# A new order for a kernel's front part: queries last, a compression on four column tiles, and attention signalled branch by branch

## The reference, cut to what matters

```
h = rms_norm(x, norm1_w) * (1 + sc1) + sh1
q, kvs, gate_logits, b_gate, c_gate, u = split(h @ w_in)
k_c = rms_norm(silu(blocks(kv0) @ w1k) @ w2k);  v_c = silu(blocks(kv1) @ w1v) @ w2v
o = g0 * softmax(q k_c + bias) v_c + g1 * softmax(q k_s + bias) v_s + g2 * softmax(q k_w + bias) v_w
y_conv = b_gate * short_conv(c_gate * u, conv_w)
x = x + g1 * (rms_norm(concat(o, y_conv)) @ w_out)
```

## Time and profile before

| what | value |
|---|---|
| median of three runs | 1794.41 us |
| the profiled execution, its own time | 1793.89 us |
| its span in the trace | 1792.1 us |
| mean granted TensorE clock | 0.882 |
| PE busy | 1398.0 us (78%) |
| DVE busy | 611.7 us (34%) |
| bytes moved | 589.96 MB, mean 329 GB/s |
| chain that ended last | DMA 48%, PE 42%, DVE 5% |

### The profile page before, as it was taken

One profiled execution on the slowest core, in us unless ns is written; L12 is line 12 of the kernel. 1 busy time (PEld: TensorE's weight loads), 2 busy tenths in 40 slices (PEclk: granted clock), 3 DMA queues, 4 the chain that ended last, 5 costly groups with the idle time before them and its releaser, 6 DMA issues.

```text
span 1792.1 us, 24506 instructions
## 1 busy us (share of the span) xinstructions
PE 1398.0 (78%) x10619; PEld 860.1 (48%) x10619; DVE 611.7 (34%) x956; ACT 199.5 (11%) x439; POOL 5.0 (0%) x10
## 2 busy tenths in 40 slices
PE   6978798675676666757676766666998999989997
PEld 4976755221222122212221122214886999879997
DVE  2654536200000000000000000006437777757785
ACT  2112322000000000000000000001332000120001
POOL 1000000000000000000000000000000000000000
PEclk8999999788888688888878798788999999989999
DMA  9789855999999999999999999995962654505541
GB/s 385 297 357 414 307 210 199 429 428 429 429 428 429 429 428 428 428 429 428 429 428 429 429 429 428 429 428 210 400 271 82 234 186 171 206 18 206 198 172 74
DMA packets 46260, 589.96 MB, mean 329 GB/s; under 512 B 5328, under 2 KB 7792, under 8 KB 9088
## 3 DMA queue, kind: packets, MB, share of 16 engines
q1 hardware_dynamic: 42464, 581.84, 78.7%
q10 hardware_dynamic: 3744, 7.37, 1.2%
HBM read 586.56 MB, written 2.62 MB: 329 GB/s over the span
## 4 chain that ended last, share of the span: by engine, by line
DMA 48%; PE 42%; DVE 5%; issue 2%; ACT 2%; SPq 0%; DVEq 0%; ACTq 0%
DMA ring<-in_w 44%; PE ps L1420 5%; PE ps L1842 4%; PE ps L1843 4%; PE ps L1847 4%; PE ps L1674 3%; PE ps L1581 3%; PE ps L1689 3%; PE ps L1364 2%; PE ps L1858 2%; PE ps L1861 2%; PE ps L1860 2%; DMA ring<-in_w_ada 1%; DVE ring_parts L747 1%; DMA ring<-in_mix_in 1%
## 5 line engine op out<-in xcount | busy, mean ns | idle before, releaser
L1674 PE MATMUL ps<-ring,mixT 128*32 128x512 f32 x2048 | 313.7, 749 | 178.9 <-DMA ring<-in_w 177.4
L1689 PE MATMUL ps<-ring,arena 128*32 128x512 f32 x1024 | 174.2, 818 | 105.7 <-DMA ring<-in_w 93.4
L1674 PEld LDWEIGHTS ps<-ring,mixT 128*32 128x32 f32 x2048 | 62.9, 123 | 401.7 <-DMA ring<-in_w 275.0
L747 DVE TENSOR_TENSOR ring_parts<-ring,ring_parts 128x1024 fp32r<-128x1024 f32 (+3 forms) x119 | 189.7, 1625 | 1.0
L1091 DVE TENSOR_TENSOR arena<-arena,ps 128x512 f32<-128x512 f32 x16 | 11.0, 688 | 512.7 <-PE ps L1674 512.5
L1842 PE MATMUL ps<-mixT_parts,ring_parts 128*128 128x256 f32 x704 | 168.0, 280 | 6.7 <-issue 6.7
L1843 PE MATMUL ps<-mixT_parts,ring_parts 128*128 128x256 f32 x704 | 167.5, 280 | 0.0
L1689 PEld LDWEIGHTS ps<-ring,arena 128*32 128x32 f32 x1024 | 33.6, 132 | 230.2 <-DMA ring<-in_w 144.3
L1842 PEld LDWEIGHTS ps<-mixT_parts,ring_parts 128*128 128x128 f32 x704 | 134.7, 191 | 8.0 <-issue 7.1
L744 DVE CAST ring_parts<-ring 128x1024 fp32r<-128x1024 f32 (+3 forms) x119 | 100.4, 891 | 105.3 <-DMA ring<-in_f 69.5
L1843 PEld LDWEIGHTS ps<-mixT_parts,ring_parts 128*128 128x128 f32 x704 | 134.7, 191 | 0.8
(11 more groups left out here) (342 smaller groups left out, 1381.1 us busy)
## 6 DMA issues: line engine op xcount, KB each, us to landing
ring<-in_w SPq DMA_DIRECT2D x192, 2048.0 KB, 26.0
ring<-in_ada_w SPq DMA_DIRECT2D x24, 2048.0 KB, 12.4
ring<-in_f SPq DMA_DIRECT2D x22, 2048.0 KB, 8.1
ring<-in_w_ada SPq DMA_DIRECT2D x12, 2048.0 KB, 13.7
ring<-in_f SPq DMA_DIRECT2D x22, 1024.0 KB, 6.4
ring<-in_w_in SPq DMA_DIRECT2D x5, 2048.0 KB, 14.4
ring<-in_w_out SPq DMA_DIRECT2D x2, 2048.0 KB, 9.8
ring<-in_mix_in SPq DMA_DIRECT2D x2, 2048.0 KB, 15.4
```

The source lines that it names most:

```text
L747: return tt(out.bitcast(F32R), v, hi, ALU.subtract)
L1674: last = mm(ps[rows[u], j, :], XeT[:, 2 * m + k, rows[u]], w[:, u, k * FE:(k + 1) * FE], start=(m == 0 and k == 0), stop=(m == 3 and k == 1))
L1689: last = mm(ps[rows[u], m, :], heT[:, k, rows[u]], w[:, u, m * 512:(m + 1) * 512], start=(k == 0), stop=(k == FE // P - 1))
```

## The change

It renumbers the ring so that ada chunks stand between the parts of w_in and the queries' part RW[0] comes last; PE, DVE and ACT follow that order. The compression puts the 16 products of a matrix on four column tiles, each of which sums four of them into its own 32 rows of PSUM; ACT copies the four partial sums, and four products with a new constant `fold` (it adds rows p with equal p % 32 and turns the result) take the place of the four transposes, silu coming after them. The squares and norm of q are done for each half of the tokens, the second half after RW[0] ends. The bias tables are made earlier. Attention is written out without loops; maxima, exponentials and transposes signal the s branch before the w branch, the copies have a semaphore for each branch, and the 12 RL0 chunks are spread anew: two before the first queries, ten between the steps. Their sum into the modulation row (`ada_half`) must be done before the third pair's queries. SP's loads of RL0 are written out too. The diff, cut:

```diff
-RA = (0, 1, 2, 3, 12, 13, 14, 15, 20, 21, 24, 25)
-RW = (4, 6, 8, 10, 16, 18)
-RC = 22
+RA = (0, 1, 2, 3, 6, 7, 10, 11, 16, 17, 20, 21)
+RW = (24, 4, 22, 8, 14, 18)
+RC = 12
...
+        blk_at = at[0] - 2 * LPAIRS * 2 * NC
+        blk32 = lambda v, m: arena[:, blk_at + (v * LPAIRS + m) * 2 * NC:blk_at + (v * LPAIRS + m) * 2 * NC + 32]
...
-            def ada_loads(l, n):
-                with sp.Fori(0, 2) as i:
-                    for s in range(NS):
-                        one = A["ada_w_2"][bass.ds(i * NS + (l * 12 + s), 1)]
-                        load(n + s, one.rearrange("c p n -> p (c n)"), CHUNK, i)
-
-            ada_loads(0, RL0)
+            for c in range(12):
+                load(RL0 + c, A["ada_w_2"][c], CHUNK)
...
+            done(act, RC + 1)
+            nc.scalar.activation(hidS, ps[:, 7, :], ACT.Copy).then_inc(hid_act, 1)
+            done(act, RW[4])
...
+            act.wait_ge(hidT_tr, 1)
+            nc.scalar.activation(hidT[:, :, 0:30], ps[:, 7, 384:512].rearrange("p (v n) -> p v n", v=4)[:, :, 0:30],
+                                 ACT.Silu).then_inc(hidT_ev, 1)
...
+            for t in range(NT):
+                if t == 0:
+                    act.wait_ge(q_first, 1)
+                else:
+                    done(act, RW[0])
+                nc.scalar.activation(q[:, t, :], ps[:, 4 + t, :], ACT.Copy).then_inc(win_act, 1)
+                act.wait_ge(head_ss, 3 + t)
+                nc.scalar.activation(sd24[:, 8 * t:8 * t + 8], SS[:, 8 * t:8 * t + 8], ACT.Sqrt, scale=1.0 / HD,
+                                     bias=epsc).then_inc(head_sd, 1)
...
+            for u in range(PAIRS):
+                if u + 1 < PAIRS:
...
+                for b in range(2):
+                    act.wait_ge(a_M, 2 * u + b + 1)
+                    for h in range(2):
...
                     last.then_inc(a_E, 1)
-                    act.wait_ge(a_T, i * 4 + (2 * u + 2))
...
+                act.wait_ge(a_T, 2 * u + 2)
+                nc.scalar.activation(PTw, ps[:, 4:6, 0:384], ACT.Copy).then_inc(a_Pw, 1)
...
             high_h(1, 2)
-            high_w(RW[0], 512)
+            high_w(RW[1], 512)
             low_h(1)
-            low_w(RW[0], 512)
-            split_w(RW[1], 512)
-            split_w(RW[2], 280)
+            low_w(RW[1], 512)
             split_w(RW[3], 512)
...
+            dve.wait_ge(win_act, 1)
+            dve.wait_ge(blk_ready, 1)
+            head_squares(0, ksv)
+            split_w(RW[4], 512)
+            ada_round(1, 6)
+            dve.wait_ge(tab_in, 32 + 16 * NH)
...
+            split_w(RW[5], 512)
+
+            dve.wait_ge(kc_mm, 1)
...
+            split_w(RW[2], 280)
...
+            done(dve, RW[5])
             dve.wait_ge(win_act, 3)
...
+            split_w(RW[0], 512)
+            ada_round(2, 6)
+
+            dve.wait_ge(win_act, 4)
+            head_squares(1, kwg)
+            dve.sem_inc(head_ss, 1)
+            dve.wait_ge(head_sd, 2)
+            link(nc.vector.reciprocal(RS[:, 16:24], sd24[:, 16:24]))
...
             dve.wait_ge(cv_sd, 1)
             link(nc.vector.reciprocal(sq, sq))
...
+            for t in range(NT):
+                qt = q[:, t, :].rearrange("p (h d) -> p h d", d=HD)
+                h8 = slice(8 * t, 8 * t + 8)
+                dve.wait_ge(win_act, 5 + t)
+                link(tt(qs, qt, qt, ALU.mult))
+                nc.vector.tensor_reduce(SS[:, h8], qs, AX.X, ALU.add).then_inc(head_ss, 1)
+                dve.wait_ge(head_sd, 3 + t)
+                link(nc.vector.reciprocal(RS[:, h8], sd24[:, h8]))
+                last = tt(qt, qt, RS[:, h8].unsqueeze(2).to_broadcast([P, 8, HD]), ALU.mult)
+            last.then_inc(q_normed, 1)
+            dve.wait_ge(k_tr, 1)
+            ts(kTs, ps[:, 2, 0:256], kn[:, 1:2], None, ALU.mult)
+            ts(kTw, ps[:, 2, 256:512], kn[:, 2:3], None, ALU.mult).then_inc(k_ready, 1)
+            done(dve, RW[0])
...
+                link(tt(split(L[:, 0:2, C1:TABW]), split(ps[:, 2:4, C1:TABW]), split(tb[:, :, C1:TABW]), ALU.add))
...
+                nc.vector.tensor_reduce(nM[:, :, 1, 0], L[:, 0:2, 0:256], AX.X, ALU.max, negate=True)
+                link(nc.vector.tensor_reduce(nM[:, :, 1, 1], L[:, 0:2, 256:384], AX.X, ALU.max, negate=True))
+                ts(nM[:, :, 0, :], nM[:, :, 0, :], -0.01 * NEG, None, ALU.min).then_inc(a_M, 1)
+                dve.wait_ge(a_w, u + 1)
                 link(tt(L[:, 2:4, 0:384], ps[:, 4:6, 0:384], tb[:, :, 0:384], ALU.add))
...
-                nc.vector.tensor_reduce(nM[:, :, 1:3, 0], Lb[:, :, :, 0:256], AX.X, ALU.max, negate=True)
-                nc.vector.tensor_reduce(nM[:, :, 1:3, 1], Lb[:, :, :, 256:384], AX.X, ALU.max, negate=True)
-                link(nc.vector.tensor_reduce(nM[:, :, 0, :], split(L[:, 0:2, C1:TABW]), AX.X, ALU.max, negate=True))
-                ts(nM[:, :, 0, :], nM[:, :, 0, :], -0.01 * NEG, None, ALU.min).then_inc(a_M, 1)
...
+                nc.vector.tensor_reduce(nM[:, :, 2, 0], L[:, 2:4, 0:256], AX.X, ALU.max, negate=True)
+                nc.vector.tensor_reduce(nM[:, :, 2, 1], L[:, 2:4, 256:384], AX.X, ALU.max, negate=True).then_inc(a_M, 1)
+
+            def probabilities(u):
+
+                dve.wait_ge(a_T, 2 * u + 1)
+                nc.vector.tensor_copy(PTs[:, :, 0:384], ps[:, 2:4, 0:384])
+                nc.vector.tensor_copy(PTs[0:47, :, 384:512], ps[0:47, 2:4, 384:512]).then_inc(a_Ps, 1)
+                dve.wait_ge(a_E, 2 * u + 2)
                 link(ts(CO, SM, 1e-30, None, ALU.max))
...
-            with dve.Fori(0, PAIRS // 2) as i:
-                link.enter(i, 14)
-                logits(i, 0)
-                probabilities(i, 0)
...
+            logits(0)
+            probabilities(0)
+            logits(1)
+            combined(0)
+            probabilities(1)
+            ada_half(0)
+            logits(2)
+            combined(1)
+            probabilities(2)
+            logits(3)
+            combined(2)
+            probabilities(3)
+            ada_half(1)
+            combined(3)
...
                 return last

             pe.wait_ge(h_split, 1)
...
+            features(RW[1], 512, 2, 2, low_parts(1, 1))
             tokens(RW[1], 512, 256, [ps[:, 3, t * 256:(t + 1) * 256] for t in range(NT)], None).then_inc(ring_used, 2)
...
+            ada_chunk(RA[4], 6, 0, 0)
+            ada_chunk(RA[5], 6, 1, 0)
+            features(RW[3], 512, 4, 0, low_parts(1, 2)).then_inc(ring_used, 2)
+            ada_chunk(RA[6], 6, 2, 0)
+            ada_chunk(RA[7], 6, 3, 0)
             pe.wait_ge(blk_ready, 1)
...
+            pe.wait_ge(zeroed, 5)
             for v in range(2):
                 arrived(RC + v)
                 w = ring_view(RC + v, LPAIRS)
...
+                for m in range(LPAIRS // 4):
+                    for j in range(4):
+                        last = mm(ps[32 * j:32 * j + 32, 7, v * CMP_HID:(v + 1) * CMP_HID], blk32(v, 4 * j + m),
+                                  w[:, 4 * j + m, :], start=(m == 0), stop=(m == LPAIRS // 4 - 1))
                 last.then_inc(ring_used, 1)
...
+            features(RW[4], 512, 4, 4, low_parts(1, 3)).then_inc(ring_used, 2)
             pe.wait_ge(hid_act, 1)
             for v in range(4):
...
+                last = mm(ps[:, 7, 384 + v * 32:384 + (v + 1) * 32], hidS[:, v * P:(v + 1) * P], C("fold"), start=True,
+                          stop=True)
             last.then_inc(hidT_tr, 1)
+            pe.wait_ge(ada_ev, 2)
+            ada_chunk(RA[8], 6, 0, 0)
+            ada_chunk(RA[9], 6, 1, 0)
             pe.wait_ge(hidT_ev, 1)
             pe.wait_ge(misc_in, 64)
             for v in range(2):
                 for p0 in ((0,) if v == 0 else (0, 32)):
                     for g in range(2):
                         for j in range(2):
...
+                            last = mm(ps[p0:p0 + NC, 7, v * P + g * HD:v * P + (g + 1) * HD],
                                       hidT[:, 2 * v + j, g * NC:(g + 1) * NC], cw2[:, v, j, :], start=(j == 0),
                                       stop=(j == 1))
             last.then_inc(kc_mm, 1)
...
+            pe.wait_ge(win_act, 2)
+            features(RW[5], 512, 4, 0, low_parts(1, 4)).then_inc(ring_used, 2)
             pe.wait_ge(kc_n, 1)
...
+            tr(ps[:, 7, 256:256 + NC], kcn[0:NC, :], ident[0:NC, 0:NC]).then_inc(kc_tr, 1)
+            ada_chunk(RA[10], 6, 2, 0)
+            ada_chunk(RA[11], 6, 3, 0)
+            pe.wait_ge(win_dve, 1)
+            tokens(RW[2], 280, 0, [ps[:, 2 + t, 0:280] for t in range(NT)], low_parts(1, 5)).then_inc(ring_used, 2)
+            pe.wait_ge(cv_sq, 1)
+            for f in range(4):
+                last = mm(ps[:, f // 2, (f % 2) * T:(f % 2 + 1) * T], C("bd"), sq[:, f * T:(f + 1) * T], start=True,
+                          stop=True)
+            last.then_inc(cv_sum, 1)
+            pe.wait_ge(win_act, 3)
+            tokens(RW[0], 512, 0, [ps[:, 4 + t, :] for t in range(NT)], low_parts(1, 6), q_first).then_inc(ring_used, 2)
```

(63 more changed lines are left out.)

277 lines of the change are left out of this document (99 added, 178 removed).

## The result

The changed kernel takes **1785.08 us** (median of five runs, 1783.09 to 1787.71) against 1794.25 us for the kernel before beside it (five runs, 1793.26 to 1795.39): a ratio of 0.995, with a 95% interval of 0.9938 to 0.9961. That is 9.2 us faster, where 23.3 were predicted, and 1785.08 lies outside the range of 1764 to 1781. The profiled execution took 1785.08 us, its span is 1783.3, so the spans of the two profiled executions (1792.1 before) differ by 8.8 us.

The account below looks back on a forecast made before the run. Expert weights' transfers bound 300 to 1230 us but hand on an earlier start; the front's chain and attention's waits set that start. Front 8.5 plus attention 14.8 is 23.3 us off 1793.9: 1770.6, stated as 1771, range 1764 to 1781.

Parts of the forecast that it names:

- Behind attention nothing changes: After attention: the next 64 us and the loads of that part keep their distances, so no time gained or lost.
- rival C: Expert stream: it swallows the gain, leaving 1794 us; chance 0.04.
- the larger constant table: Constants' load: stands beside longer work, as do SP's unrolled loads and the gate's sigmoid; no cost.
- The front, 8.5 us: Before attention: the replayed new order brings the first scores from 158.8 to 150.3 us, 8.5 us less.
- rival A: Front: gives nothing, as loads land later beside btab's scattered traffic and DVE's tail grows; 1779 us, chance 0.13.
- what is late next is DVE: End of the front: DVE's queue, with the 6.55 us reciprocal ahead of two query halves, has q ready at 145.3.
- Attention, 14.8 us: Attention: 61.5 us against 76.3, 14.8 us less, of which 3.8 are the two chunks moved ahead.
- the clock's term: Attention: 1.5 us allowed for PE at the low clock, with one 3.1 us wait left; bounds 0 and 5.8.
- Rival D: Attention: PE held at the low level throughout, slower, 1827 us with all four pairs; chance 0.03.
- The split maxima: Attention on DVE: two more reductions a pair cost 0.3 us; 1.2 us taken back if all four are on the path.
- Unrolling, 0 us: PE's attention code doubled: code loading taken as 0, bounds below 0 and 6.8 us.
- B: Compression: its products do not run side by side on the column tiles; 1773 us, chance 0.06.

Follow-up runs that it names:

- e1: The changed kernel with the 32 fold columns in a tile of their own behind the arena, every other tile where it lay before the change: 1781.7 us.
- e2: The kernel before with 32 unused columns added to its constants, nothing else: 1801.5 us.
- e16: The kernel before with an unused tile of 32 columns ahead of hT, moving hT, mixT and all behind by 128 bytes: 1800.07 us in one run.
- e9: e1 without the bias table's way through memory (write of btab and its skewed reads left out; biases not the reference's): 1775.66 us in one run.
- e14: e1 with the compression's 32 products one behind another on 32 output rows, as before the change: 1778.97 us in one run.
- e12: e1 with the convolution's reciprocal in halves, one between the query halves on DVE, the other behind the first queries' scaling: 1773.27 us.
- e7: e1 with constants and vectors behind the arena, no tile ahead of x; hT and mixT at 128 modulo 256 bytes: 1791.87 us.
- e10: e1 with two ada chunks computed earlier, in PE's idle time at 34 us, ahead of w_in 1: 1777.33 us.
- e11: e1 with constants and vectors behind the arena, ctxcol ahead of x; hT and mixT at 192 modulo 256 bytes: 1790.28 us in one run.
- e3: The kernel before with the changed attention alone, front and constants as they were, two ada chunks ahead of the first queries: 1779.9 us.
- e6: e1 with constants and vectors behind the arena, modcol ahead of x; hT and mixT at 0 modulo 256 bytes: 1791.49 us.

## Why the prediction was wrong

**"Behind attention nothing changes ... the loads of that part keep their distances": this step failed, and it is 7.4 of the 14.1 us missing (14.5 by the profiled spans: 7.4 in the FFN, 8.1 in the front, 0.8 between attention and the experts, less 1.8 that attention gave beyond its forecast).** The expert stream kept its distance to the tenth (1076.9 us), and handed on the earlier start, as the first reading said; rival C is out. But the diff has a line that moves data in every later stage: "the larger constant table" was priced only as a transfer that stands beside longer work. It shifts hT and mixT by 128 bytes, and 2112 products of the FFN (22 x 96) pay 3.5 ns each; taking the shift back (e1) gave 7.4 us, making it alone cost 6.2 and 6.4 (e2, e16). The stated limit of 2 us from the first expert product to the end was passed (1493.1 to 1500.5), and so was the one of 155 for the first scores (158.45).

**The front, 8.5 us: this step failed too, by 8.1.** The replay had RW[4]'s products end at 97.7; the chain has them at 106.7, and from there to the first scores the replay, with its 1.7 us, has 52.6 and the trace 51.8. So the stretch behind was priced right as a whole, and the 9.0 us arose ahead. They are four terms of the replay: RW[3] ended at 73.3 instead of 70; RW[4] took 15.0 us to land instead of 11.6; the split 0.2 more; its products 11.5 instead of 9.4. Two things stand behind them. One is the clock, which the replay left at the full level through the whole front: RW[1]'s last 80 products took 11.2 us at 0.85 instead of the 9.4 priced, which is 1.9 of the first term, and of RW[4]'s 80 the first 24 took 4.7 us where the next 24 took 2.8, which is 1.9 of the fourth. Some 3.8 of the 9.0 us are thus a term put at nothing; in e1, where RW[4]'s products ran at the full clock, they took 9.7. The other is the landing, the second term, which rival A named as btab's scattered traffic: without it the load landed at 84.5 and not 88.3 (e9), and 1.8 us of that reached the scores. A further 1.1 us is that RW[1]'s second group of products began at 46.9 and not at 45.8. What the replay did foresee came true: the compression gives nothing by itself (its bound was 1.7 us; e14 shows 0.8 at most), its 64 records take 3.9 us as priced, at the pace of the tiled expert products, and "what is late next is DVE" was right, and bigger than I used: with the reciprocal moved out of the way the same front is worth 6.6 us (152.2 against 158.8, e12). I had seen that the reciprocal stands ahead of both query halves and did not ask what moving it would give.

**Attention, 14.8 us: right in the main, and 16.6 measured** (59.7 us instead of 61.5). Pair by pair 14.0, 14.6, 14.0 and 17.1 us, against 12.5, 15.3, 14.7 and 17.5, and 1.5 for the clock. That the first pair is 1.5 us over its price, just the clock's term, is luck. The low level cost it 4.1 us, 2.4 in the scores (5.2 instead of 2.75) and 1.7 in the ada chunk (3.64 instead of 1.9), and the waits for the exponentials, priced at 3.8, were 1.2, since PE itself was slower beside them. The place was wrong too: the term was hung on the wait for the exponentials, but the level fell ahead of attention, where PE waited for DVE, and PE was wholly busy for 8.6 us before it rose, by 168 us. Rival D did not happen: from 168 us to the end of attention the clock was 1.00. The size is also one of two that the runs show: with the 61.5 us of e1, e7, e10 and e11 (first score to last value product, 76.1 before) the gain would read 14.6. Alone, in the kernel before, the changed attention gave 13.3 us (e3, 1793.2 to 1779.9).

**The split maxima.** After, two reductions of 512 elements and two of 256 a pair stand for one of 1024 and one of 512:

```profile
L944 DVE TENSOR_REDUCE small<-arena 128x2 f32<-128x512 f32 x4 | 2.7, 677 | 0.0
L945 DVE TENSOR_REDUCE small<-arena 128x2 f32<-128x256 f32 x4 | 1.6, 410 | 0.0
```

2 x 0.68 and 2 x 0.41 are 2.18 us against 1.22 + 0.68 in the earlier trace rows: 0.28 more a pair, the 0.3 priced. The Trainium skill (VectorE: DVE Perf Modes, The TRN2 errata) has such a fixed cost per instruction, and the rows agree; on the path it did not count, since PE waited only 1.2 us for all exponentials together.

**The other signs that were named.** The granted clock in attention is 0.92, not above 0.95, since the stretch begins at the low level; the compression's own work is under 4 us; the long reciprocal ended at 150.0, some 1.8 us behind RW[0]'s products. The stretch to the first expert product lost 0.8 us: the router's products (L1657) took 6.2 us, at a clock of 0.66 in those ten microseconds, against 3.8 before.

**Unrolling, 0 us**: held within what the traces can show. PE has one stop of 0.95 us that nothing explains, just ahead of the last values, and the FFN's pace follows data and not code (e3).

**The rivals.** A gave 1779 for a front worth nothing, and had the chance of 0.13. Its outcome happened, a front that gave 0.4 us, and the late landing was part of it; but DVE's part did not grow (51.8 us behind RW[4]'s products against 52.6), and the clock, which it did not name, weighed as much. With the 7.4 us of the FFN its time reads 1786, near the 1785.08 measured. B, C and D did not happen. No rival asked what else in the diff reaches past its own stage.

## What to carry to other kernels

A diff's smallest line can be its dearest: list every tile whose address moves, since an untouched loop that runs 2000 products reads them too, and try the same kernel with a few unused columns before and after its main operands. Replaying an order with loads through a ring, an error at one load is kept or handed to the next by the slots, so price the landing by the transfers that are then in flight, small-packet ones included, and ask for every load that PE waits for whether the products behind it will run at the full clock. And when an engine's queue is last, look first at its longest instruction whose result is needed later than what stands behind it; moving one reciprocal brought the first scores 5.3 us forward (e12), more than the whole new front did (0.4 in the changed kernel, 2.8 between e3 and e1).

## What the runs showed of the hardware

- A float32r product of 256 columns streaming a tile took 276 ns (records) where the tile began at 64 modulo 256 bytes of the partition, 279 or 280 at 192 and 96, 283 and 284 at 128 and 0: 416 to 426 us from the first FFN product to the end, and a granted clock of 1.00 in the steps read. What a page says on it: the Trainium skill (SBUF — State Buffer, Operand start alignment) wants a float32 operand to start at a multiple of 4 bytes, as a matter of legality alone; all these do. Whether the tile's distance to the ring, which began at 128 modulo 256 in all runs, or the address itself is what counts was not tried, nor was the mechanism.
- Kernels with the same attention ran the 20 us from 210 at a clock of 1.00 (the changed kernel, e6, e9) or 0.83 (e1, e7, e10, e11), and from the first scores to the first expert product e1 took 4.4 us longer than the changed kernel. A difference of that size between two variants need not be the variants' own.
- A load of 2 MB (RW[4]) landed between 87.2 and 89.8 us in ten kernels whether it went out at 72.0 or at 78.3, and at 84.5 in the one without the 2.5 MB of 1 to 1.5 KB packets (e9).
- Products behind a wait of PE ran at the low level: sixteen products of 256 columns took 3.78 us at a granted clock of 0.50, after waits of 5.38 and 0.68 us, and 2.05 at 1.00.
- Four column tiles brought 64 records of 256 columns from 14.0 us to 3.9 (e14 and after), a factor of 3.6.
